# Modulated transposes stay in their PSUM bank

## The reference

```
mod = (silu(c) @ w_mod[l] + b_mod[l])            # sh1, sc1, ga1, sh2, sc2, ga2
h = rmsnorm(x, g_pre_mix[l]) * (1 + sc1) + sh1   # modulation, ahead of the mixer
m = mixer(h)                                     # h @ w_in, latent attention and spatial gating, merged @ w_out
x = x + ga1 * rmsnorm(m, g_post_mix[l])
h = rmsnorm(x, g_pre_ffn[l]) * (1 + sc2) + sh2   # modulation, ahead of the feed-forward part
f = (silu(h @ w_gate[l]) * (h @ w_up[l])) @ w_down[l]
x = x + ga2 * rmsnorm(f, g_post_ffn[l])
```

## Time and profile before

| | |
|---|---|
| median of 3 runs | 3808.58 us (3808.47 to 3809.55) |
| span of the profiled execution, first to last instruction | 3804.7 us |
| TensorE matmul busy | 3386.0 us, 89% |
| VectorE busy | 1797.6 us, 47% |
| ScalarE busy | 1038.8 us, 27% |
| GpSimd busy | 1426.3 us, 37% |

### The profile page before, as it was taken

One profiled execution on the slowest core, in us unless ns is written; L12 is line 12 of the kernel. 1 busy time (PEld: TensorE's weight loads), 2 busy tenths in 40 slices (PEclk: granted clock), 3 DMA queues, 4 the chain that ended last, 5 costly groups with the idle time before them and its releaser, 6 DMA issues. The chain is left out here.

```text
span 3804.7 us, 48831 instructions
## 1 busy us (share of the span) xinstructions
PE 3386.0 (89%) x19532; PEld 3033.0 (80%) x19532; DVE 1797.6 (47%) x2807; ACT 1038.8 (27%) x2298; POOL 1426.3 (37%) x804
## 2 busy tenths in 40 slices
PE   5998888888999998999988978888899999899997
PEld 2987677767888888888878777776788888888886
DVE  3116777754444534534433156786443453453333
ACT  2323555553100001200014234776320110120001
POOL 2210687810654544444530302000054454455441
PEclk7998899989999999999999988998999999999998
DMA  6205444422322223322222134112232222242222
GB/s 202 71 15 160 143 146 147 150 78 88 101 74 77 72 73 89 99 69 72 73 60 100 55 123 119 29 34 67 76 117 72 67 74 77 72 131 75 72 67 67
DMA packets 397728, 337.90 MB, mean 89 GB/s; under 512 B 107192, under 2 KB 325000, under 8 KB 397504
## 3 DMA queue, kind: packets, MB, share of 16 engines
q1 hardware_dynamic: 249808, 233.18, 20.1%
q10 hardware_dynamic: 147696, 101.61, 9.2%
HBM read 282.87 MB, written 51.87 MB: 88 GB/s over the span
## 5 line engine op out<-in xcount | busy, mean ns | idle before, releaser
L581 POOL TENSOR_SCALAR w_hi<-raw 128x1024 fp32r<-128x1024 f32 (+2 forms) x400 | 458.7, 1147 | 2270.2 <-PE ps L598 2135.0
L583 POOL TENSOR_TENSOR w_lo<-raw,w_hi 128x1024 fp32r<-128x1024 f32 (+2 forms) x400 | 975.4, 2438 | 33.4
L596 PE MATMUL ps<-w_lo,ht_hi 128*128 128x512 f32 (+2 forms) x2040 | 798.5, 391 | 145.8 <-DVE tokm L1685 83.3
L596 PE MATMUL ps<-ht_lo,w_hi 128*128 128x320 f32 x2816 | 873.3, 310 | 4.9 <-DVE ht_lo L1359 3.0
L597 PE MATMUL ps<-ht_hi,w_lo 128*128 128x320 f32 x2816 | 871.6, 310 | 0.0
L598 PE MATMUL ps<-ht_hi,w_hi 128*128 128x320 f32 x2816 | 871.5, 309 | 0.0
L597 PE MATMUL ps<-w_hi,ht_lo 128*128 128x512 f32 (+2 forms) x2040 | 787.1, 386 | 0.0
L598 PE MATMUL ps<-w_hi,ht_hi 128*128 128x512 f32 (+2 forms) x2040 | 784.9, 385 | 0.0
L596 PEld LDWEIGHTS ps<-w_lo,ht_hi 128*128 128x128 f32 x2040 | 397.8, 195 | 232.5 <-DVE tokm L1685 99.0
L596 PEld LDWEIGHTS ps<-ht_lo,w_hi 128*128 128x128 f32 x2816 | 530.0, 188 | 8.1 <-DVE ht_lo L1359 3.8
L597 PEld LDWEIGHTS ps<-ht_hi,w_lo 128*128 128x128 f32 x2816 | 530.0, 188 | 1.6
(11 more groups left out here) (127 smaller groups left out, 3681.2 us busy)
## 6 DMA issues: line engine op xcount, KB each, us to landing
raw<-in_w_gate_dram SPq DMA_DIRECT2D x88, 512.0 KB, 3.8
raw<-in_w_up_dram SPq DMA_DIRECT2D x88, 512.0 KB, 3.8
raw<-in_w_down_dram SPq DMA_DIRECT2D x88, 512.0 KB, 3.5
raw<-in_w_mod_dram SPq DMA_DIRECT2D x80, 512.0 KB, 4.3
x_rows<-tokm ACTq DMA_DIRECT2D x30, 512.0 KB, 5.0
x_old<-x_rows ACTq DMA_DIRECT2D x30, 512.0 KB, 4.3
kv_rows<-stage ACTq DMA_DIRECT2D x20, 512.0 KB, 3.3
tokm<-kv_rows ACTq DMA_DIRECT2D x30, 320.0 KB, 4.1
```

The source lines that it names most:

```text
L581: pool.tensor_scalar(hi, r, 1.0, 0.0, ALU.mult, ALU.add).then_inc(s_whi, 1)
L583: pool.tensor_tensor(lo, r, hi.bitcast(F32), ALU.subtract).then_inc(s_w, 1)
L596: pe.matmul(out, lhs[0], rhs[1], start=first, stop=False)
```

## The change

ScalarE writes scale and shift back into the PSUM bank from which it reads, and no longer waits for VectorE. VectorE reads the bank in both of its instructions. TensorE waits, whatever the name of tile n - 2, for VectorE's signal before it transposes into the bank again. The numbers computed are the same.

```diff
                 if n >= 2:
-                    last = tb_keys[n - 2][0]
-                    pe.wait_ge(s_tbm if last in ("mix", "ffn") else s_ht, n - 1)
+                    pe.wait_ge(s_ht, n - 1)
...
                 b = after_product(act, key)
-                if n >= 2:
-                    act.wait_ge(s_ht, n - 1)
                 w = groups[gi][1] * P
-                act.activation(tbank[:, n % 2, 0:w], ps[:, b, 0:w], ACT.Identity, bias=shift, scale=scale).then_inc(s_tbm, 1)
+                act.activation(ps[:, b, 0:w], ps[:, b, 0:w], ACT.Identity, bias=shift, scale=scale).then_inc(s_tbm, 1)
...
                 dve.wait_ge(s_tbm, n + 1)
-                src = tbank[:, n % 2, 0:nt * P]
+                src = ps[:, plan[key][0], 0:nt * P]
                 link(dve.tensor_copy(hi, src))
                 dve.tensor_tensor(lo, src, hi.bitcast(F32), ALU.subtract).then_inc(s_ht, 1)
```

## The result

The changed kernel takes 3829.14 us (median of four runs, 3826.1 to 3832.16), the kernel before 3808.52 beside it: the ratio is 1.0049, 95% interval 1.0036 to 1.0061. In a second series of six runs it took 3827.59, ratio 1.0045 (1.0033 to 1.0058). So the change costs 18 to 21 us where +8.0 was forecast; the direction was right, the time lies above the range. The profiled execution took 3832.16 us, its span is 3830.4.

The account below looks back on a forecast made before the run. TensorE, busy 89% of the span, bounds the kernel, so the change counts where TensorE waits. Gains -9.6 plus costs 17.6 give +8.0 us on the median 3808.58: 3816.6 us, own range 3813 to 3822, range for all 3805 to 3822.5.

Parts of the forecast that it names:

- the price of each instruction: Modulated tile of 512 columns: activation stays 0.78 us, PSUM cast 0.69, subtraction 0.69; VectorE 1.34 us instead of 1.06.
- Rival 3: PSUM cast costs what the SBUF cast costs, 0.42 us: -2.8 us, 3805.8, no change; chance 0.09.
- rival 4: VectorE's new pair still stalls against GpSimd, so the gains go: 3826 us; chance 0.04.
- between the halves: Burst between the feed-forward halves, four tiles of 384 and four of 256: product starts 2.15 us later, two layers, +4.3.
- the pairs: Pairs of tiles between products in later token groups: +0.7 for 512 columns, +0.6 for 256.
- Rival 1: Rings close sooner: a round a tenth shorter, 0.3 us, costs 13 instead of 17.6: 3812, no tellable change; chance 0.24.
- the gains: First bursts of both layers, where GpSimd splits weights: -6.7 and -2.9 us, together -9.6.
- the costs: Slower tiles elsewhere, where GpSimd is quiet: 0.7 + 0.6 + 2.0 + 6.6 + 4.3 + 3.4 = 17.6 us.
- the feed-forward part: The 24 tiles inside the feed-forward loops cost nothing, since TensorE waits for none of their low halves before the next boundary.
- rival 2: Freed VectorE time in the feed-forward part shrinks the wait for line 1685: up to -33 us, 3784; chance 0.05.
- the step on TensorE's clock: Extra time at TensorE's lower clock left at zero, judged from the burst ending at 955.5; at most +4 us.
- the triples: Output projection, three tiles after two of 512 in the same banks: transposes wait +0.5 us, four places, +2.0.

Follow-up runs that it names:

- filled kernels: Changed kernel and kernel before, each with extra identity transposes on TensorE in its waits: 3805.01 us (again 3808.71) and 3804.33 us (again 3803.65).
- first bursts only: Against the kernel before, only the twelve tiles of both layers' first bursts stay in PSUM, the other 100 keep the SBUF buffer: 3802.29 us, ratio 0.9984.
- filled kernel before: The kernel before with extra identity transposes on TensorE in its own waits: 3804.33 us, ratio 0.9989; again 3803.65 us, ratio 0.9981.

## Why the prediction was wrong

**Right: the price of each instruction.** The activation takes 0.75 us, the cast 0.69, the subtraction 0.69, and none stretches. Rival 3 (a cast of 0.42 us) and rival 4 (stalls stay) fall. One reading behind the choice of 0.69 isn't right as told: 0.42 us for 512 columns leaves room for 0.105 us per 128, of which 0.137 is 1.3 times and not twice. Twice it is against the step between the SBUF casts of 512 and 128 columns (0.42 and 0.22 us, 0.067 per 128).

**Right: the waits.** Each burst moved by what its round gave, in sum +8.6 for +8.0. Two terms were off by more than half a us: between the halves +5.75 for +4.3, because a round of 256 columns took 2.30 us (1476.45 to 1478.75) and not 1.98, with 0.66 us for two transposes at the lower clock, and the pairs +0.7 for +1.3. Rival 1 (shorter rounds) falls. The whole runs show less of both sides: at equal time at the lower level the gains are 6.2 us for 9.6 and the costs 11.5 for 17.6, so that part of the match of the sums is luck.

**Right: the feed-forward part gives nothing.** Line 1682 keeps its 83.4 us, so rival 2 falls, although those 24 tiles cost VectorE less than before. What VectorE saves there, nobody had waited for.

**Wrong: the step on TensorE's clock.** It said "I leave this at zero, since it restarts low before and after", at most +4. It looked at one burst, whose stretch at the lower level was indeed as long before and after (10.2 us). The same burst in the second layer has 13.7 us after and 10.2 before, and the place between the halves 10.2 and 6.8 in both layers, alike in both profiles of each kernel. In all the runs show 22 to 30 us more at the lower level, by the line through the runs about 9 us of time; of what the change costs the eight stretches, filling takes back 14.7 - 7.9 = 6.8 us. What failed is the step from a clock that is low before and after to nothing lost: at three of the four places with a longer burst the clock also stayed low longer, and in the second layer's output projection, with this burst and the triples' longer waits, it was low for 31 us in both profiles after, 17 and 21 in those before. Forecast and this term make +17, of the +18 to +21 measured. That the clock takes the larger part of what is missing is shown by the filled kernels, which give back 22 us on the changed kernel and 5 to 6.5 on the one before; how the missing 10 to 13 us divide by place is an estimate.

**Open.** Two untouched feed-forward passes of the first layer ran at the lower level in both profiles of the changed kernel, worth some 3 us there, with waits as long as before. Since first bursts only lost as much in the second layer, where none of its waits is longer, that those passes belong to the change isn't shown. Why the clock fell in just those, and whether attention takes part, isn't settled.

## What to carry to other kernels

A wait that is made longer on a TensorE that is 89% busy has two prices, the wait itself and the clock behind it, and here the second was about as large as the first: read the granted clock behind every wait that a change lengthens, also where it is full before, and in more than one execution. Dropping the buffer paid here only where VectorE's stalls beside GpSimd were on the path, in 12 of 112 tiles, which alone make the kernel 0.16% faster. And 299 transposes that nobody reads, put into the waits, gave back about all that the change had cost; the kernel before gained 5 to 6.5 us by such transposes too.

## What the runs showed of the hardware

- Transposes of fp32 data kept the granted clock at 1.00 through a wait behind which it had been 0.50 (136 to 146 us filled, 140.4 to 143.6 unfilled, above): 299 of them took the time at the lower level from some 388 to 320 us.
- An activation that writes its own PSUM bank is a little faster than one into SBUF: 748 ns for 775 at 512 columns, 432 for 458 at 128.
- Identical executions differ by attention alone from 434.7 to 448.0 us (two profiles of the filled kernel before, granted clock 0.93 and 0.91 there): one profile cannot tell a few us there.
- A half-speed microsecond costs 0.37 us by the runs, less than the half that the ratio of the clock's levels would give. That the rest is hidden behind other engines is an inference; no run tests it.
